# Queries and keys of the second block, turned by VectorE in 32x32 blocks instead of by TensorE

## What is computed

```python
h = rmsnorm(x, g_mix)
proj = h @ w_in          # qa ka va | qb kb vb | fl | qc kc vc | qi ki wi | gates
br_a = stick_breaking_attention(qa, ka, va)      # 8 heads of 64
log_f = log_sigmoid(fl + b_forget)
br_b = forgetting_attention(qb, kb, vb, log_f)   # 8 heads of 64
qc, kc, qi, ki = partial_rope(...)               # the only rotated ones
br_c = indexed_sparse_attention(qc, kc, vc, qi, ki, wi, top_k=64)
y = sum(sigmoid(gate_i) * (br_i @ w_branch[i]))
x = x + y @ w_out
x = x + square(relu(rmsnorm(x, g_mlp) @ w_up)) @ w_down
```

## Time and profile before

| | us |
|---|---|
| median of 3 runs | 1802.46 (1802.33 to 1802.56) |
| the profiled execution | 1802.23 |
| its span, first to last instruction | 1800.3 |
| TensorE busy | 1781.4 |
| GpSimd busy | 1360.7 |
| ScalarE busy | 1047.0 |
| VectorE busy | 760.9 |

### The profile page before, as it was taken

How to read it: one execution, slowest core, us unless ns; L and a number is a source line. 1 busy time by engine, 2 the same in 40 slices (tenths; PEclk the granted TensorE clock), 3 DMA queues, 4 the chain that set the end, 5 groups by cost and what they waited for, 6 DMA issues and landing times.

```text
span 1800.3 us, 25383 instructions
## 1 busy us (share of the span) xinstructions
PE 1781.4 (99%) x9224; PEld 1488.8 (83%) x9224; DVE 760.9 (42%) x1340; ACT 1047.0 (58%) x1560; POOL 1360.7 (76%) x573
## 2 busy tenths in 40 slices
PE   7999999999999999999999999999999999999998
PEld 4888888888888888888888878898888888888887
DVE  2782344843334446343338374321112665431112
ACT  4645675445677654466665666555555566746554
POOL 5867787866778877676879766778888865688886
PEclk9999999999999999999999999999999999999999
DMA  9975556754556677455647544556665644456663
GB/s 368 313 232 164 164 176 210 237 154 136 158 180 188 175 208 232 137 152 150 194 135 223 152 130 140 175 172 191 188 190 175 190 143 133 146 179 196 187 186 129
DMA packets 171409, 327.88 MB, mean 182 GB/s; under 512 B 10416, under 2 KB 15792, under 8 KB 171312
## 3 DMA queue, kind: packets, MB, share of 16 engines
q1 hardware_dynamic: 168272, 320.49, 58.0%
q10 hardware_dynamic: 3040, 6.06, 1.0%
HBM read 325.46 MB, written 1.05 MB: 181 GB/s over the span
## 4 chain that ended last, share of the span: by engine, by line
PE 69%; POOL 15%; issue 14%; DMA 1%; ACT 0%; POOLq 0%; DVE 0%; SPq 0%; ACTq 0%; DVEq 0%
PE G L1892 16%; PE G L1894 16%; PE G L1893 16%; POOL wlo L525 15%; PE A L2601 3%; PE G L2601 2%; PE A L1892 2%; PE A L1894 2%; PE A L1893 2%; PE A L2602 1%; PE G L2602 1%; PE A L2344 1%; PE G L2366 1%; DMA raw<-in_w_in 1%; PE A L1946 1%
## 5 line engine op out<-in xcount | busy, mean ns | idle before, releaser
L525 POOL TENSOR_TENSOR wlo<-raw,whi 128x1024 fp32r<-128x1024 f32 (+1 forms) x568 | 1357.0, 2399 | 425.6 <-ACT whi L550 423.1
L550 ACT ACTIVATE whi<-raw 128x1024 fp32r<-128x1024 f32 (+1 forms) x568 | 593.4, 1048 | 570.3 <-PE G L1894 427.4
L1892 PE MATMUL G<-whi,hparts 128*128 128x512 f32 (+1 forms) x1472 | 581.9, 395 | 1.0 <-DVE hparts L1278 0.6
L1894 PE MATMUL G<-whi,hparts 128*128 128x512 f32 (+1 forms) x1472 | 568.1, 386 | 0.0
L1893 PE MATMUL G<-wlo,hparts 128*128 128x512 f32 (+1 forms) x1472 | 567.8, 386 | 0.0
L1892 PEld LDWEIGHTS G<-whi,hparts 128*128 128x128 f32 x1472 | 276.5, 188 | 59.1 <-issue 5.2
L1894 PEld LDWEIGHTS G<-whi,hparts 128*128 128x128 f32 x1472 | 276.3, 188 | 57.1
L1893 PEld LDWEIGHTS G<-wlo,hparts 128*128 128x128 f32 x1472 | 276.8, 188 | 50.8
L1892 PE MATMUL G<-whi,osplit 128*128 128x512 f32 x240 | 94.2, 393 | 0.0
L1894 PE MATMUL G<-whi,osplit 128*128 128x512 f32 x240 | 93.4, 389 | 0.0
L1893 PE MATMUL G<-wlo,osplit 128*128 128x512 f32 x240 | 93.4, 389 | 0.0
(11 more groups left out here) (413 smaller groups left out, 2554.4 us busy)
## 6 DMA issues: line engine op xcount, KB each, us to landing
raw<-in_w_in SPq DMA_DIRECT2D x324, 512.0 KB, 3.8
raw<-in_w_up SPq DMA_DIRECT2D x64, 512.0 KB, 3.7
raw<-in_w_down SPq DMA_DIRECT2D x64, 512.0 KB, 3.5
raw<-in_w_out SPq DMA_DIRECT2D x40, 512.0 KB, 3.9
raw<-in_w_branch_out SPq DMA_DIRECT2D x36, 512.0 KB, 4.4
modw<-in_w_mod SPq DMA_DIRECT2D x32, 512.0 KB, 5.0
raw<-in_w_branch SPq DMA_DIRECT2D x24, 512.0 KB, 3.5
modz<-in_w_mod SPq DMA_DIRECT2D x16, 512.0 KB, 9.8
```

Of the source, the lines that this page charges most:

```text
L525: pool.tensor_tensor(wlo[:, s, :, 0:n], raw[:, s, :, 0:n], whi[:, s, :, 0:n].bitcast(F32), ALU.subtract)\
L550: act.activation(whi[:, slot, :, 0:n], raw[:, slot, :, 0:n], ACT.Copy).then_inc(hi_ready, 1)
L1892: pe.matmul(bank, hi, whi[:, slot, kk, 0:n], start=first, stop=False)
L1894: return pe.matmul(bank, lo, whi[:, slot, kk, 0:n], start=False, stop=last)
```

## The change

qa, ka, qb and kb are no longer turned by TensorE. VectorE turns them with `turn_heads`: for each of the four, 16 instructions, one per pair of a token group of 32 and a feature group of 32, each with 32 partitions x 256 elements (2 tiles x 4 blocks x 32), read from `z2` and written straight to `t2`, both in SBUF. It does so after `memset(fgw)` and before it waits for `forget_log`, each after the evacuation of its chunk. `BESIDE` keeps only the pairs 8 to 12. The factor 1/8 of the queries goes into ScalarE's evacuation of QA and QB through a new `rstd_q` (= 1/(8 rms)), computed by two small VectorE instructions and waited for by ScalarE with `query_scale`. TensorE waits for four `heads_turned` before the cumulative sum.

```diff
--- before.py
+++ after.py
@@ -274,6 +274,7 @@
         bag = sb("bag", [P, TT, 2])
         dev = sb("dev", [P, TT])
         rstd_sq = sb("rstd_sq", [P, TT])
+        rstd_q = sb("rstd_q", [P, TT])
 
         gate2 = [sb_at(f"gate2_{n}", [P, TT, CH], F32, at) for n, at in enumerate((
             zb + 33792, zb + 37888, tb + 25600, place["cx"], place["cx"] + 4096))] + [gate2_5]
@@ -359,6 +360,7 @@
         sm_scores, sm_max, sm_exp, sm_turned, sm_copied = (sem(n) for n in (
             "sm_scores", "sm_max", "sm_exp", "sm_turned", "sm_copied"))
         sm_normed, heads_out = sem("sm_normed"), sem("heads_out")
+        query_scale, heads_turned = sem("query_scale"), sem("heads_turned")
         last_rstd, out_scaled = sem("last_rstd"), sem("out_scaled")
         up_done, up_copied, up_summed = sem("up_done"), sem("up_copied"), sem("up_summed")
         ff_relu, ff_sq, ff_done, out_ready, out_stored = (sem(n) for n in (
@@ -385,8 +387,7 @@
 
 
 
-        BESIDE = {(2, 1): (0,), (2, 2): (1,), (3, 0): (2,), (3, 1): (3,), (3, 2): (4,), (3, 3): (5,),
-                  (4, 0): (8, 9), (4, 1): (10, 11, 12), (4, 2): (6, 7)}
+        BESIDE = {(4, 0): (8, 9), (4, 1): (10, 11, 12)}
         MOD_ORDER = (0, 2, 1, 3)
         HALVES = [[(c, s) for c in range(3) for s in part] for part in ((0, 1), (2, 3))]
         MOD_FIRST = {(1, 1): 3, (2, 0): 1, (2, 1): 4, (0, 3): 1, (1, 3): 1, (2, 3): 1}
@@ -1001,11 +1002,13 @@
                         dst = t2[:, 2 * n:min(2 * n + 2, 25)].rearrange("p b s -> p (b s)")
                         act.wait_ge(turned, w(turned))
                         act.activation(dst, A[turns["n"] % 4][:, 0:dst.shape[-1]], ACT.Copy,
-                                       scale=DH ** -0.5 if n // 2 in (0, 2, 4) else 1.0).then_inc(turned_copied, 1)
+                                       scale=DH ** -0.5 if n // 2 == 4 else 1.0).then_inc(turned_copied, 1)
                         turns["n"] += 1
 
+                act.wait_ge(query_scale, w(query_scale))
                 for c, col in enumerate(SECOND):
-                    evacuate((c + 1) % 2, [z2[:, t, col:col + CH] for t in range(TT)], ACT.Copy, scale,
+                    evacuate((c + 1) % 2, [z2[:, t, col:col + CH] for t in range(TT)], ACT.Copy,
+                             [rstd_q[:, t:t + 1] for t in range(TT)] if col in (QA, QB) else scale,
                              beside=lambda s, c=c: copy_beside(c, s))
 
                 for h in range(NI):
@@ -1665,12 +1668,23 @@
             def gained_low(a, l, quarters):
                 turned_low(lambda k: gT[:, a, bass.ds(l, 1), k], None, HB_OUT, quarters)
 
+            def turn_heads(dst, col):
+
+                for i in range(P // PART):
+                    for j in range(P // PART):
+                        rows, feats = slice(i * PART, (i + 1) * PART), slice(j * PART, (j + 1) * PART)
+                        ins = dve.transpose(dst[feats].rearrange("p h (t s) -> p t h s", t=TT)[:, :, :, rows],
+                                            z2[rows, :, col:col + W].rearrange("p t (h f) -> p t h f", f=P)[:, :, :, feats])
+                ins.then_inc(heads_turned, 1)
+
             def layer(l):
                 if l == 0:
                     second_tile_low(l)
                 else:
                     gained_low(0, l, (2, 3))
                 token_scale()
+                link(dve.tensor_scalar(rstd_q[:], rms[:, 0:TT], DH ** 0.5, None, ALU.mult))
+                dve.reciprocal(rstd_q[:], rstd_q[:]).then_inc(query_scale, 1)
                 dve.wait_ge(evacuated, w(evacuated, 2 * TT + 3 * TT))
 
                 for t in range(TT):
@@ -1695,11 +1709,14 @@
                 link(dve.tensor_scalar(fg[:, 2], fg[:, 0], 0.0, None, ALU.min))
                 dve.memset(fgw[:], 0.0).then_inc(dve_step, 1)
                 dve.wait_ge(dve_step, w(dve_step))
+                for a, col in enumerate((QA, KA, QB, KB)):
+                    dve.wait_ge(evacuated, w(evacuated, TT))
+                    turn_heads(t2[:, 4 * a:4 * a + 4], col)
                 dve.wait_ge(forget_log, w(forget_log))
                 for n in range(3):
                     ins = dve.tensor_tensor(fgw[:, :, n, 0:NF], fg[:, 2], fg[:, 1], ALU.subtract)
                 ins.then_inc(forget_ready, 1)
-                dve.wait_ge(evacuated, w(evacuated, 5 * TT))
+                dve.wait_ge(evacuated, w(evacuated, TT))
 
                 link(dve.tensor_scalar(wis[:], z2[:, :, WI:WI + NI], NI ** -0.5 * DH ** -0.5, None, ALU.mult))
                 tiles = [slice(0, P), slice(P, 3 * P)]
@@ -2417,8 +2434,6 @@
                     for n in BESIDE.get((c, s), ()):
                         if n == 8:
                             pe.wait_ge(roped, w(roped))
-                        if n in (4, 6):
-                            pe.wait_ge(evacuated, w(evacuated, TT))
                         m = turns["n"]
                         if m >= 4:
                             pe.wait_ge(turned_copied, w(turned_copied))
@@ -2430,8 +2445,7 @@
 
                 for c in range(len(SECOND)):
                     p = (c + 1) % 2
-                    if c < 4:
-                        pe.wait_ge(evacuated, w(evacuated, TT))
+                    pe.wait_ge(evacuated, w(evacuated, TT))
                     for s in range(SLOTS):
                         slab(G[2 * p:2 * p + 2], *h_pairs, s)
                         turn_beside(c, s)
@@ -2448,7 +2462,8 @@
                       .then_inc(idx_dots, 1)
                 for n in range(LATE_FIRST):
                     late_slab(n, G[0:2])
-                pe.wait_ge(evacuated, w(evacuated, TT))
+                pe.wait_ge(evacuated, w(evacuated, 2 * TT))
+                pe.wait_ge(heads_turned, w(heads_turned, 4))
 
                 pe.wait_ge(idx_summed, w(idx_summed))
                 pe.wait_ge(forget_ready, w(forget_ready))
```

## The result

| | before | after |
|---|---|---|
| median, same chip and time | 1802.4 us (4 runs) | 1816.95 us (1812.86, 1816.76, 1817.15, 1817.4) |
| ratio to before | | 1.0076 [1.0063, 1.0089] |
| profiled execution, its span | 1802.23, 1800.3 us | 1817.4, 1815.5 us |
| measured again at another time | 1802.34 us (12 runs) | 1816.49 us (1816.06 to 1817.1, 4 runs), ratio 1.0079 [1.0061, 1.0097] |

The kernel became slower by 14.5 us; 1815.8 was forecast. The first part of the page after answers to the earlier trace rows.

The account below looks back on a forecast made before the run. TensorE, busy 1781.4 of 1800.3 us, was taken as the bound. Removed work -7.8, stalls +17.2 and clock +4 gave +13.4 us on 1802.2, so 1815.6, forecast as 1815.8 us for the median; 8-in-10 range 1797 to 1824.

Parts of the forecast that it names:

- Removed: TensorE's 32 removed transposes a layer, ahead of the cumulative matmul: 3.88 us a layer earlier, 7.8 us for two.
- One transpose: Each of the 64 added VectorE transposes a layer takes 0.44 us without overlap, 28.2 us a layer.
- C: Rival theory in the experiments: the loss comes from GpSimd stretching VectorE's transposes; no chance given.
- rival (d): VectorE's transposes wait for GpSimd like the rope operations: stall of 27.6 us a layer, 1854 us; chance 0.07.
- The start: Layer 0's VectorE transposes start near 998.4 instead of 991.05, since earlier GpSimd subtractions block the duplications ahead of them.
- layer 1's "1432": Sign to look for: layer 1's first VectorE transpose starts near 1432, not 1424.
- The stall: TensorE, ready at 1021.87, waits for idx_summed at 1030.45 before the cumulative matmul: 8.6 us a layer, 17.2 us.
- The chain: VectorE's forget logits, weighted sums and mask up to idx_summed, behind the transposes: 3.85 us with GpSimd resting, 5.88 before.
- The clock: After each stall TensorE's granted clock falls: 2 us a stall, 4 us in all, 7 at most.
- Rival (a): Transposes start undelayed at 991.05: stalls of 1.2 to 3.2 us a layer, no clock price, 1797 to 1801 us; chance 0.17.

Follow-up runs that it names:

- half: Changed kernel, but only QA and KA turned by VectorE; QB and KB turned by TensorE and copied by ScalarE as before: 1798.24 us, ratio to before 0.9977.
- dup_act: Changed kernel with the eight duplications (copies into `dup`) done by ScalarE instead of VectorE, after KB's second slab: 1805.78 us, ratio to before 1.0021.
- rope12: Changed kernel with both token tiles rotated in one pass, 12 VectorE rope operations instead of 24: 1800.74 us, ratio to before 0.9991.
- busy2: Changed kernel with 56 unread extra TensorE matmuls ahead of its waits for heads_turned and idx_summed: 1810.22 us, ratio to before 1.0049.
- pairs: Changed kernel with QA and KA, and QB and KB, turned together: 32 transposes of 32x512 a layer instead of 64: 1805.47 us, ratio to before 1.0021.
- busy: Changed kernel with 56 unread extra TensorE matmuls behind its wait for heads_turned: 1821.6 us, ratio to before 1.0109.
- idle_turns: Kernel before, its TensorE transposes kept, plus 64 VectorE transposes a layer into a spare area nobody reads: 1806.2 us, ratio to before 1.0022.

## Why the prediction was right

- **Removed, 3.88 us a layer.** The first dots start at 1009.07 instead of 1013.08, the last slab's matmuls end at 1021.9 where L2456 was put at 1021.87, and half measured the half of it, 1.95.
- **One transpose, 0.44 us.** 436 ns a record, 0.450 from start to start, so 28.83 us a layer for 28.2. Nothing overlaps. With this the quadrant rule of the Trainium skill (VectorE: DVE Perf Modes, "Two Vector instructions with no wait between them") agrees, and so does the estimate of 444 ns from its table. None of the 128 is stretched (443 ns at most) beside the subtractions, so C and rival (d) fall, which is what the Trainium skill's page SBUF — State Buffer, "Who interferes with whom", says of instructions with at most one SBUF input outside the two-port modes.
- **The start, 998.4.** 997.6, by the mechanism that was worked out: two duplications pass by 987.2, then one or two after each subtraction (989.5, 991.8, 994.4). The inner division was off: all eight are done by 994.6, not after 997.2, and then a forget operation waits until 997.1, which the sum had let pass freely. dup_act takes the duplications away and rope12 puts them 5.6 us earlier, and in both the start of layer 0 goes to 987.6. One thing I overlooked in what would show it: layer 1's "1432" left out what layer 0's stall adds. It is 1439.1, which is 997.8 in the coordinates of layer 0 (433.44 + 4.84 of later cumulative matmul + 3.0 of clock).
- **The stall, 8.6 us a layer.** 8.69 and 8.75. The chain is 3.86 us (1026.47 to 1030.33) for 3.85. That it came so near is partly luck: the start was put 0.8 us too late and the 64 transposes 0.6 us too short, and the two cancel.
- **The clock, 2 us a stall.** The term that was mis-sized: 3.0 and 2.3 us in the first profile, 5.3 in all instead of 4, inside the bound of 7. TensorE's matmuls run at the low level for 5 to 6 us there, longer than the start of the run had made me think. In the second profile of the same kernel, where it is some 4 us, the price is 2.2 and 2.1, close to the 2 that I took. busy2 shows that it is a price of its own.
- **Rival (a)** was worked out too cheap, for two reasons. The chain is not 3.85 us long while GpSimd works: in the changed kernel GpSimd's last subtractions before the stall run from 1015.22 to 1020.04 and from 1020.36 to 1022.74. With a start at 991.05 the transposes would end at 1019.9. Those of dup_act and rope12 end at 1016.4 and their chain at 1023.7, those of busy2 end at 1021.6 and their chain at 1026.7. An estimate from these rows is an idle time of 2 to 5 us a layer, -3.8 to +2.2 us in all, so 1798 to 1804 instead of 1797 to 1801, before any clock. And such an idle time is not too short for the clock, as I had it: it fell behind 1.94 us in rope12 and in pairs, and cost 1.5 us. My lower end of the range, 1797, rested on this rival and was too low. No run has just this start.

Against the profiled execution the sum was 1815.6, and 1817.4 was measured. Of the 1.8 us between, 0.2 lie in the stalls, 1.3 in the clock and none in what was removed; 0.3 is what the three measured terms leave open.

## What to carry to other kernels

When work is moved to an engine that has idle time, put the moved instructions on that engine's own timeline, ahead of whatever is queued behind them, and compare the new end with the time at which the bounding engine asks for it: here 28.8 us went into a gap of 27.3, and the 3.9 us a layer gained on TensorE made the same gap shorter and, by moving GpSimd's work, pushed the start back by 6.6. Where small operations of one engine each wait for a long one of another, as VectorE's rope operations do here for GpSimd's subtractions, their price goes by their number and not by their size (2.52 us with 160 elements, 2.44 with 80), so merging them (24 to 12) bought 16.2 us, more than the 11.5 of merging the transposes. A stall of the bounding engine that makes its clock fall costs more than itself: 2.1 to 3.0 us on 8.7 here, and 1.5 on 1.9.

## What was not expected of the hardware

- **Which operations get into a gap varies.** In layer 0 of busy, busy2 and pairs, whose code up to the transposes is that of the changed kernel, all eight duplications passed in one gap and the transposes began at 992.8; in both profiles of the changed kernel and in half they were blocked one by one or in twos, and the transposes began at 997.6 to 997.75. In layer 1 of busy2 and pairs they were blocked as well. Of busy2's timeline, layers 0 and 1:

```profile
986.55 0.23 DVE L1700 COPY dup<-z 128x128 f32<-128x128 f32 x1
...
987.41 0.19 DVE L1702 COPY dup<-z 128x64 f32<-128x64 f32 x1
987.51 2.47 DVE L1706 TENSOR_TENSOR fg<-z,small 128x8 f32<-128x8 f32 x2
...
1423.64 2.39 DVE L1702 COPY dup<-z 128x64 f32<-128x64 f32 x1
```

  The last rope operation ended there, in layer 0, 0.3 us earlier than in the changed kernel. It may be why times spread: 6 to 8 us in idle_turns, dup_act, pairs and busy, 1.5 in rope12, and a single run of the change at 1812.86. That was not shown run by run, and it can't be the duplications alone, since dup_act has none on VectorE and spreads the most.
- **An idle time of 2 us can cost the clock, and need not.** The granted clock fell to 0.50 behind 1.94 us of idle time in layer 0 of pairs and in layer 1 of rope12, both times after TensorE had been at work again for about 1 us, and each time it cost about 1.5 us. It stayed at 1.00 behind 1.97 and 1.95 us in layer 0 of rope12 and dup_act, behind 2.03 in busy2 and 1.78 (twice) in idle_turns. What decides is not shown.
- **The chain's length depends on GpSimd.** From the forget subtractions to the mask it takes 3.86 us when GpSimd rests, 5.88 before, and in the runs where GpSimd is at work 5.0 (busy2) to 8.0 (pairs). A stall so shortens the chain that ends it.
- **A 32x512 transpose costs 0.717 us, a 32x256 one 0.450:** 0.267 for 256 elements per partition and, by these two sizes, 0.18 fixed.
